# Chunked RWKV-7 scan: block inverses on four 32x32 quarters of the TensorE array instead of two 64x64 halves

## What is computed

```python
def wkv7_scan(r, w, k, v, kk, a, reverse):
    B, S, H, N = r.shape
    def step(state, inp):
        r_t, w_t, k_t, v_t, kk_t, a_t = inp
        sa = jnp.einsum('bhvk,bhk->bhv', state, -kk_t)
        state = (state * w_t[:, :, None, :] + sa[..., None] * (kk_t * a_t)[:, :, None, :]
                 + v_t[..., None] * k_t[:, :, None, :])
        return state, jnp.einsum('bhvk,bhk->bhv', state, r_t)
```

## Time and profile before

| | |
|---|---|
| median of 3 runs | 2738.7 us (2731.55 to 2768.6) |
| profiled execution | 2732.23 us |
| its span, first to last instruction | 2730.4 us |
| instructions in the trace | 52,710 |
| TensorE busy | 2433.9 us (89%) |
| DVE, ACT, POOL busy | 1595.7, 1062.4, 677.5 us |
| mean granted TensorE clock | 0.93 |

### The profile page before, as it was taken

One profiled execution on the slowest core, in us unless ns is written; L12 is line 12 of the kernel. 1 busy time (PEld: TensorE's weight loads), 2 busy tenths in 40 slices (PEclk: granted clock), 3 DMA queues, 4 the chain that ended last, 5 costly groups with the idle time before them and its releaser, 6 DMA issues. The chain is left out here.

```text
span 2730.4 us, 52710 instructions
## 1 busy us (share of the span) xinstructions
PE 2433.9 (89%) x22191; PEld 1962.5 (72%) x22191; DVE 1595.7 (58%) x2165; ACT 1062.4 (39%) x1865; POOL 677.5 (25%) x498
## 2 busy tenths in 40 slices
PE   5799999999994999999979889998997994999990
PEld 2488887788884999999869756665876883666760
DVE  4444469966652354555445566666886445677756
ACT  5311133344441345445445455554122220555542
POOL 1122245545432345434213320001200000000004
PEclk8899999999995699999869989999998995999995
DMA  8422234443324132332043391103755123999977
GB/s 360 172 77 78 78 106 146 142 158 133 140 110 156 45 88 69 88 92 65 19 133 109 101 326 51 33 24 113 245 164 195 69 70 140 400 422 418 414 298 300
DMA packets 178735, 433.31 MB, mean 159 GB/s; under 512 B 38298, under 2 KB 90298, under 8 KB 160834
## 3 DMA queue, kind: packets, MB, share of 16 engines
q1 hardware_dynamic: 148548, 323.10, 34.1%
q0 software_dynamic: 15840, 57.54, 5.5%
q10 hardware_dynamic: 14112, 49.29, 4.5%
HBM read 307.15 MB, written 122.73 MB: 157 GB/s over the span
## 5 line engine op out<-in xcount | busy, mean ns | idle before, releaser
L99 PE MATMUL ps_in<-h_t_low,w_in_high 128*128 128x512 f32 x960 | 379.6, 395 | 10.5 <-POOL w_in_low L490 10.5
L100 PE MATMUL ps_in<-h_t_high,w_in_low 128*128 128x512 f32 x960 | 374.6, 390 | 0.0
L101 PE MATMUL ps_in<-h_t_high,w_in_high 128*128 128x512 f32 x960 | 374.6, 390 | 0.0
L99 PEld LDWEIGHTS ps_in<-h_t_low,w_in_high 128*128 128x128 f32 x960 | 180.7, 188 | 53.0 <-POOL w_in_low L490 11.5
L1191 POOL TENSOR_TENSOR wkv_levels<-wkv_nt,level_mask 128x1024 f32<-128x1024 f32 x60 | 140.1, 2353 | 274.5 <-ACT wkv_nt L1140 274.5
L101 PEld LDWEIGHTS ps_in<-h_t_high,w_in_high 128*128 128x128 f32 x960 | 180.6, 188 | 38.2
L100 PEld LDWEIGHTS ps_in<-h_t_high,w_in_low 128*128 128x128 f32 x960 | 180.8, 188 | 36.0
L2963 DVE TENSOR_TENSOR w_low<-w_now,w_high 128x2048 fp32r<-128x2048 f32 x64 | 146.7, 2292 | 39.3 <-ACT w_high L2800 39.3
L598 ACT COPY p_row<-ps_in 128x512 f32<-128x512 f32 x72 | 42.3, 588 | 304.5 <-PE ps_in L101 278.9
L2670 POOL DMA_INDIRECT xb<-h,row_ids x34 | 32.9, 967 | 511.1 <-PE ps_xy L2715 285.4
L488 POOL CAST w_in_high<-w_in_tile 128x1024 fp32r<-128x1024 f32 x40 | 46.6, 1164 | 335.8 <-PE ps_in L101 299.5
(11 more groups left out here) (383 smaller groups left out, 5788.9 us busy)
## 6 DMA issues: line engine op xcount, KB each, us to landing
w_now<-in_w SPq DMA_DIRECT2D x68, 1024.0 KB, 9.5
w_tile<-in_w SPq DMA_DIRECT2D x34, 1024.0 KB, 9.4
w_ada_tile<-in_w_ada SPq DMA_DIRECT2D x12, 2048.0 KB, 12.3
wkv_in<-wkv_out SPq DMA_DIRECT2D x24, 1024.0 KB, 3.9
w_in_tile<-in_w_in SPq DMA_DIRECT2D x40, 512.0 KB, 3.6
yb<-yb_tile ACTq DMA_DIRECT2D x34, 512.0 KB, 9.3
yb<-att_zeros POOLq DMA_DIRECT2D x32, 512.0 KB, 18.2
p_t<-p_mixed ACTq DMA_DIRECT2D x24, 512.0 KB, 2.7
```

The costliest lines, as they stand in the source:

```text
L99: nc.tensor.matmul(out, w[0], x[1], start=start, stop=False)
L100: nc.tensor.matmul(out, w[1], x[0], start=False, stop=False)
L101: return nc.tensor.matmul(out, w[0], x[0], start=False, stop=stop)
```

## The change

The two off-diagonal 32x32 blocks of a level matrix are zero, so the change computes only the diagonal ones. `lmask`, `nt`, `lev` and `z` become 32 columns wide, `level_z` and `level_xz` become 64 matmuls with 32x32 operands on the four quarters with equal row and column (`quads`), and `keep_z` is one copy. `keep_nt` copies the diagonal blocks alone, with four copies of 32 partitions instead of two of 64. `half_product` takes its off-diagonal block from `lbm` instead of `nt`, and `keep_nt` no longer waits for `half_full`. `level` and `first_inverse` have half of the elements, and `first_inverse` one step instead of two. The host's mask is folded to 32 columns.

```diff
@@ level_z, level_xz (TensorE)
                 for h in range(2 * H):
-                    for c in range(2):
-                        mm = nc.tensor.matmul(LV[half(c), 0, h], lev[half(c), l, h], x[half(c), i % 2, h], start=True, stop=True)
+                    for a in quads:
+                        mm = nc.tensor.matmul(LV[a, 0, h], lev[a, l, h], x[a, i % 2, h], start=True, stop=True)
...
-                    for c in range(2):
-                        mm = nc.tensor.matmul(LV[half(c), 1, h], z[half(c), h], xt[half(c), i % 2, h], start=True, stop=True)
+                    for a in quads:
+                        mm = nc.tensor.matmul(LV[a, 1, h], z[a, h], xt[a, i % 2, h], start=True, stop=True)
@@ half_product (TensorE)
-                            mm = nc.tensor.matmul(LV[b, 0, H * d + h], nt[a, i % 2, H * d + h, BLK * (1 - d):BLK * (1 - d) + BLK], x[a, i % 2, H * d + h],
-                                                  start=True, stop=True)
+                            at = CH * c + BLK * (1 - d)
+                            mm = nc.tensor.matmul(LV[b, 0, H * d + h], lbm[a, i % LB, 2 * d + c, h, at:at + BLK], x[a, i % 2, H * d + h], start=True, stop=True)
@@ keep_z, keep_nt (ACT)
-                nc.scalar.mul(z[:, :, 0:BLK], LV[:, 0], blk[:, 0:1])
-                nc.scalar.mul(z[:, :, BLK:CH], LV[:, 0], blk[:, 1:2]).then_inc(m["z_kept"], 1)
+                nc.scalar.copy(z[:], LV[:, 0]).then_inc(m["z_kept"], 1)
...
-                    act.wait_ge(m["half_full"], i - 1)
                     act.wait_ge(m["lev_ready"], LEVELS * (i - 1))
                 for c in range(2):
-                    ins = nc.scalar.copy(nt[half(c), i % 2].rearrange("p (d h) t -> p d h t", d=2),
-                                         lbm[half(c), i % LB].rearrange("p (d c) h t -> p d c h t", d=2)[:, :, c, :, CH * c:CH * c + CH])
+                    for b in range(2):
+                        at = CH * c + BLK * b
+                        ins = nc.scalar.copy(nt[quad(c, b), i % 2].rearrange("p (d h) t -> p d h t", d=2),
+                                             lbm[quad(c, b), i % LB].rearrange("p (d c) h t -> p d c h t", d=2)[:, :, c, :, at:at + BLK])
@@ level, first_inverse (POOL)
-                nc.gpsimd.tensor_tensor(lev[:, l], nt[:, i % 2], lmask[:, l].unsqueeze(1).to_broadcast([P, 2 * H, CH]), ALU.mult).then_inc(m["lev_ready"], 1)
+                nc.gpsimd.tensor_tensor(lev[:, l], nt[:, i % 2], lmask[:, l].unsqueeze(1).to_broadcast([P, 2 * H, BLK]), ALU.mult).then_inc(m["lev_ready"], 1)
...
-                nc.gpsimd.tensor_tensor(xt[:, i % 2], ident32[:].unsqueeze(1).to_broadcast([P, 2 * H, BLK]), lev[:, 0, :, 0:BLK], ALU.subtract).then_inc(m["x1_part"], 1)
-                pool.wait_ge(m["x1_part"], i + 1)
-                nc.gpsimd.tensor_tensor(xt[:, i % 2], xt[:, i % 2], lev[:, 0, :, BLK:CH], ALU.subtract).then_inc(m["xt_first"], 1)
+                nc.gpsimd.tensor_tensor(xt[:, i % 2], ident32[:].unsqueeze(1).to_broadcast([P, 2 * H, BLK]), lev[:, 0], ALU.subtract).then_inc(m["xt_first"], 1)
```

More of the change, by code:

```diff
@@ L792, in wkv_scan @@
         mask = s.sb("tri_mask", [P, 2, 3, CH])
-        lmask = s.sb("level_mask", [P, LEVELS, CH])
+        lmask = s.sb("level_mask", [P, LEVELS, BLK])
         ident32 = s.sb("ident_blocks", [P, BLK])
@@ L801, in wkv_scan @@
         lbm = s.sb("wkv_lbm", [P, LB, 4, H, P])
-        nt = s.sb("wkv_nt", [P, 2, 2 * H, CH])
-        lev = s.sb("wkv_levels", [P, LEVELS, 2 * H, CH])
+        nt = s.sb("wkv_nt", [P, 2, 2 * H, BLK])
+        lev = s.sb("wkv_levels", [P, LEVELS, 2 * H, BLK])
         x = s.sb("wkv_x", [P, 2, 2 * H, BLK])
         xt = s.sb("wkv_xt", [P, 2, 2 * H, BLK])
-        z = s.sb("wkv_z", [P, 2 * H, CH])
+        z = s.sb("wkv_z", [P, 2 * H, BLK])
         half_inv = s.sb("wkv_half_inverse", [P, 2 * H, BLK])
@@ L819, in wkv_scan @@
         names = ("consts_in", "v_turned", "v_kept", "bk_turned", "bk_kept", "products", "lbm_ready", "nt_ready",
-                 "mv_full", "mv_kept", "lev_ready", "x_ready", "xt_ready", "x1_part", "xt_first",
+                 "mv_full", "mv_kept", "lev_ready", "x_ready", "xt_ready", "xt_first",
                  "z_full", "z_kept", "xz_full", "half_full", "half_kept", "cross_full", "inv_parts", "inv_ready",
@@ L842, in quad @@
             return slice(64 * c + 32 * b, 64 * c + 32 * b + 32)
+        quads = [quad(c, b) for c in range(2) for b in range(2)]
         def hh(g, f):
@@ L3198, in more_layouts @@
     j, t = np.arange(P)[:, None] % CH, np.arange(CH)[None]
-    out["level_mask"] = np.array([((j >> l) ^ (t >> l)) == 1 for l in range(LEVELS)], np.float32).transpose(1, 0, 2).copy()
+    out["level_mask"] = np.array([((j >> l) ^ (t >> l)) == 1 for l in range(LEVELS)], np.float32).transpose(1, 0, 2)
+    out["level_mask"] = np.ascontiguousarray(out["level_mask"].reshape(P, LEVELS, -1, BLK).sum(2))
     out["ident_blocks"] = np.tile(np.eye(BLK, dtype=np.float32), (P // BLK, 1))
```

## The result

The changed kernel takes 2848.5 us (median of 4 runs, 2842.2 to 2853.0) against 2740.2 us (median of 4) of the kernel before on the same chip: a ratio of 1.038, with a 95% interval of 1.031 to 1.045. The forecast was 2785 us, with a range up to 2828: the right sign, half of the size, and a measured time 20 us above the range. The profiled execution took 2848.6 us and its span 2846.7, 116.3 us more than before. All of it lies in the scan. DVE's last sum into `wkv_y_tile` starts at 1490.35 us; before it started at 1374.58, so it comes 115.8 us later, and the rest of the run is merely shifted.

A forecast was written before the change was run, and what follows sets the result against it. TensorE's own stream bounds the kernel; afterwards its instruction queue would. Scan end 861.3 + 144 x 3.4 + 11 x 3.5 + 25.4 = 1414.8 against 1376.0, +39 us, +50 with the clock: 2785 us, range 2710 to 2828.

The forecast's parts named there:

- The packets (225): TensorE's instruction queue: 12,288 more records, 48 more packets on top of 177, some 225 in all.
- the work of a cycle at the full clock: One outer-loop turn of the scan: engines alone would need 38.2 - 5.0 + 0.3 = 33.5 us.
- the level group: `level_z` or `level_xz` on TensorE: 1.32 us at full clock against 1.95, 5.0 us less a cycle.
- ACT and POOL beside the path: Copies and level matrices on ACT and POOL: their changes lie beside TensorE except at the start.
- the earlier start: Scan start: three POOL operations of 1.26 us end at about 861.3, so level work begins 3.4 us earlier.
- the place of the idle time: TensorE in each cycle: "issue" idle of 8 us or more, mostly within or behind level groups.
- late packets: Instruction packets in the scan starting late behind tile loads, once or twice a cycle: 3.5 us a cycle, bounds nothing and 5.4.
- the queue can run ahead: Rival on instruction fetch: 3.2 to 3.5 us spacings were mere demand; -80, 2655 us; chance 0.22.
- binds only beside loads: Rival on instruction fetch: about 2.8 us when asked early; -35, 2700 us; chance 0.18 shared with slow quarters.
- the new form isn't as fast: Rival on level groups: 15 ns a record, group 1.9 us; -30 if queue doesn't bind; chance 0.18, shared.
- At 3.4 us that is 41.5 us.: Instruction supply of a scan cycle: 12.2 packets at 3.4 us each, more than the engines' 33.5 and today's 38.2.
- While the queue is the bound a slower engine mostly fills time it would idle away: TensorE's half clock after idle time in the scan: 1 us a cycle, from 0 to 2.

The follow-up runs named there:

- The bursts: Kernel before plus three bursts of small matmuls ahead of the scan: 2821 us including the bursts; a second kernel put dense matmuls between small ones, no total given.
- the first burst: Kernel before with bursts ahead of the scan: the opening 512 matmuls of 32x32 on the quarters, without other traffic; that kernel took 2821 us in total.
- the small loads: Changed kernel with alpha/rho and beta/kappa tile loads cut to one sixteenth from the fourth unit on: 2828.0 us, ratio 1.035.
- half-record kernel: Changed kernel with one matmul for two heads in each level group, 32 matmuls a group instead of 64: 2667.8 us, ratio 0.975.

## Why the forecast had the sign and half of the size

*What held.* The packets (225), the work of a cycle at the full clock (33.7 us for 33.5), the level group (1.22 for 1.32), ACT and POOL beside the path, the earlier start (861.4 for 861.3) and the place of the idle time ("mostly within or behind level groups"). Its size (9.1 us a cycle for 8 to 12) agrees in part by luck: supply and late packets together (45.5 + 2.6 us) lie 14.4 us above the 33.7 of work, and the low clock added 9.0 us of busy time, of which 5.3 filled that gap and 3.7 made the cycle longer. The bursts bear out the supply by packets of 256 records with less than two in store. Of the three rivals, "the queue can run ahead" fell with the first burst, "binds only beside loads" with the small loads, and "the new form isn't as fast" with the row of 1.22 us.

*What failed.* Cycles took 51.8 us, not 44 to 47. The forecast had 41.5 + 3.5 + 1 = 46 for them. Term by term:

- "At 3.4 us that is 41.5 us." The 3.4 was read from two single spacings at the fast end of what occurs (3.2 to 3.5), and the bursts show 3.6 to 3.7: 12.3 packets at 3.7 are 45.5 us, 4.0 more. This is the largest single part of the miss. I had taken the spacings that I could bracket in the rows for the typical ones.
- "I take 1.3 times 2.7, 3.5 us a cycle" for late packets: 2.6 measured by the small loads, 0.9 less.
- "While the queue is the bound a slower engine mostly fills time it would idle away; I take 1 us a cycle, from 0 to 2." What is left of 51.8 is 3.7 us; by subtraction it is the clock's, together with whatever the two other terms leave out. Two estimates from the side agree. The intervals between packets give 3.9 us. And at half clock throughout, even with fewer columns, a cycle takes 57.4 us. A clock of 0.79 means 42% of the time at half; if those stretches go at that pace, the rest goes at 48.4 us a cycle (1/51.8 = 0.42/57.4 + 0.58/48.4), and the clock costs 3.4 us. The step fails because "the queue is the bound" holds at the full clock only. At half clock a packet's worth of records takes the engine longer than the queue in many places (the 44 intervals of 4.7 us), so the bound changes place and both losses are paid, one after the other.

5.8 us a cycle times ten units are 58 of the 66 us by which the scan ended later than the forecast's 1425.8 us (1491.7, where 1490.35 is the start of the last sum of 1.39 us); the other 8 lie in the first unit, the last cycle and the last unit (27.7 us from 1464.0 on, 25.4 forecast). The split is measured for the packets and only estimated for the clock; a run with full work and the clock held up wasn't to be had, since the work that raised it (0.90) takes time itself. Two sums of the rivals are slightly off: 2738.7 less 80 and less 35 are 2659 and 2704, not 2655 and 2700; nothing hangs on it.

The two rules of the Trainium skill: the first (TensorE: Matmul & The Clock Gate, "Wait — 56ns, not 53.3ns?") would have put start-to-start at 25 ns or more; the rows have 1.22 us for 128 pairs, 9.5 ns, so the measurement decides against it for 32x32 operands on quarters. The second (Runtime: NRT & Kernel Launch, "Instruction fetch mechanics") gives TensorE room for 2048 instructions; the first burst, without other traffic, stalled after 213 pairs, 426 records, and from then on after each 256. Of that section the block of 256 held, and so did its remark that this memory is only two lines of 16 KiB; the room of 2048 didn't.

## What to carry to other kernels

Count instructions like bytes: here TensorE gets 256 records in 3.6 to 3.7 us, about 70 a microsecond, and a float32 matmul is four of them, so in a long row of such matmuls one that runs in less than 57 ns is paid by its fetch and not by its size (an estimate from that rate). Here cutting matmuls into smaller ones paid where the engine ran at half clock and had few other instructions (the first unit, 15 us of 54), and cost time elsewhere, even where the average demand was still under the supply. Where "issue" stands in the midst of a group of small matmuls, look at the spacing of the packets of the instruction queue and at the granted clock behind the stall, and take the rate from a burst, not from the fastest spacing seen.

## What the runs showed that I had not expected

- Removing three quarters of the columns in six groups of matmuls, with the instructions kept, ended the scan 59 us later than in the changed kernel, with the granted clock at 0.50 for eight units on end.
- Added dense work of some 6.8 us a cycle was nearly free (2861.0 for 2848.5 us; ratios 1.043 and 1.038, whose intervals overlap).
- The instruction packet's round trip doesn't depend on TensorE's clock (3.74 us at full, 3.6 at half), and beside full DMA queues it grows to 5.7 to 6.2 us.
- In the half-record kernel the first unit's clock was 0.90, where the changed kernel had 0.71 and the one before 0.50.
